# Two-layer decoder trunk on one core: the last mLSTM head takes its projection groups three to a chunk, and the mixer outputs are converted between its last chunks

## The reference, cut to what matters

```python
z = rms_norm(x, norm_g) @ w_in             # q, k, v, output gate o, gates
...
h = mlstm_chunkwise(q, k, v, li, lf)       # 4 heads, sequential over chunks
h = rms_norm(h, out_g)                     # per head
h = h * sigmoid(o)
return h @ w_out                           # the output projection
```

## Time and profile before

| | us |
|---|---|
| median of 3 runs | 2363.09 |
| lowest and highest | 2362.88 to 2363.49 |
| the profiled execution's own time | 2363.16 |
| its span | 2361.0 |

### The profile page before, as it was taken

One profiled execution on the slowest core, in us unless ns is written; L12 is line 12 of the kernel. 1 busy time (PEld: TensorE's weight loads), 2 busy tenths in 40 slices (PEclk: granted clock), 3 DMA queues, 4 the chain that ended last, 5 costly groups with the idle time before them and its releaser, 6 DMA issues.

```text
span 2361.0 us, 26713 instructions
## 1 busy us (share of the span) xinstructions
PE 2297.2 (97%) x10488; PEld 1878.4 (80%) x10488; DVE 1248.3 (53%) x1184; ACT 572.6 (24%) x854; POOL 898.7 (38%) x401
## 2 busy tenths in 40 slices
PE   6999999999999999999999999989999999999999
PEld 5777768888888888888777787778888888888887
DVE  8765684355545555555662443353645555544553
ACT  5445442211111111111333333332211111111110
POOL 2221225634344343434731322246344343443432
PEclk9999999999999999999998999999999999999999
DMA  4211103111111111111311111121111111111112
GB/s 157 61 38 35 41 19 116 45 54 45 54 44 52 45 45 53 44 54 51 116 37 57 44 61 54 36 107 46 53 45 46 52 44 53 44 53 45 46 53 81
DMA packets 36911, 131.47 MB, mean 56 GB/s; under 512 B 4568, under 2 KB 4952, under 8 KB 36832
## 3 DMA queue, kind: packets, MB, share of 16 engines
q1 hardware_dynamic: 34384, 121.72, 16.8%
q10 hardware_dynamic: 2448, 8.65, 0.9%
HBM read 117.73 MB, written 8.42 MB: 53 GB/s over the span
## 4 chain that ended last, share of the span: by engine, by line
PE 91%; DVE 4%; ACT 2%; POOL 2%; issue 1%; DMA 0%; SPq 0%; ACTq 0%; POOLq 0%; DVEq 0%
PE pj L1260 41%; PE dn L1280 17%; PE pj L324 16%; PE pj L303 6%; PE dn L1328 2%; PE dn L631 1%; PE pj L655 1%; PE pj L1328 1%; POOL ssum L389 1%; PE dn L1698 1%; PE pj L641 1%; PE dn L1726 1%; PE pj L463 1%; PE dn L1735 1%; PE dn L1729 1%
## 5 line engine op out<-in xcount | busy, mean ns | idle before, releaser
L1526 POOL TENSOR_TENSOR w_hi<-w_raw,ones 128x1024 fp32r<-128x1024 f32 x188 | 359.6, 1913 | 1421.0 <-PE pj L1260 569.5
L1528 POOL TENSOR_TENSOR w_lo<-w_raw,w_hi 128x1024 fp32r<-128x1024 f32 x188 | 474.7, 2525 | 14.8
L1369 DVE SCALAR_TENSOR_TENSOR ffn_y<-ffn_h,params,ffn_y 128x1024 f32<-128x1024 f32 x176 | 324.1, 1842 | 117.4 <-ACT ffn_y L1377 109.6
L1377 ACT ACTIVATE ffn_y<-ffn_h,params 128x1024 f32<-128x1024 f32 x88 | 109.6, 1245 | 885.5 <-DVE ffn_h L1358 885.5
L1358 DVE TENSOR_TENSOR ffn_h<-pj,rms_bc 128x1024 f32<-128x1024 f32 x88 | 107.8, 1225 | 365.1 <-PE pj L1260 351.5
L1418 DVE TENSOR_TENSOR res<-dn,res 128x1024 f32<-128x1024 f32 x144 | 176.1, 1223 | 115.4 <-PE dn L1280 115.4
L1260 PE MATMUL pj<-xa_hi,w_hi 128*128 128x512 f32 x704 | 216.9, 389 | 0.0
L1260 PE MATMUL pj<-xb_hi,w_hi 128*128 128x512 f32 x704 | 216.9, 389 | 0.0
L1260 PE MATMUL pj<-xa_lo,w_hi 128*128 128x512 f32 x704 | 216.8, 389 | 0.0
L1260 PE MATMUL pj<-xb_hi,w_lo 128*128 128x512 f32 x704 | 216.7, 389 | 0.0
L1260 PE MATMUL pj<-xa_hi,w_lo 128*128 128x512 f32 x704 | 216.7, 389 | 0.0
(11 more groups left out here) (265 smaller groups left out, 3395.0 us busy)
## 6 DMA issues: line engine op xcount, KB each, us to landing
w_raw<-weights SPq DMA_DIRECT2D x189, 512.0 KB, 3.5
x_first<-x_t SPq DMA_DIRECT2D x8, 512.0 KB, 9.6
res<-x_t SPq DMA_DIRECT2D x8, 512.0 KB, 7.4
scratch<-res ACTq DMA_DIRECT2D x8, 512.0 KB, 2.6
res<-scratch SPq DMA_DIRECT2D x8, 512.0 KB, 6.5
y_t<-res ACTq DMA_DIRECT2D x8, 512.0 KB, 2.6
q_turned<-q_raw SPq DMA_DIRECT2D x16, 128.0 KB, 2.3
k_turned<-k_raw SPq DMA_DIRECT2D x16, 128.0 KB, 2.3
```

The costliest lines, as they stand in the source:

```text
L1369: dve.scalar_tensor_tensor(y[:, :], h[:, SH - lag:SH - lag + S], f.tap(j, m, q), y[:, :], ALU.mult, ALU.add).then_inc(taps[f.l], 1)
L1377: act.activation(f.y[m][:, :], f.h[m][:, SH:SH + S], ACT.Identity, bias=f.tap(j, m, 3), scale=f.tap(j, m, 2)).then_inc(center[f.l], 1)
L1526: pool.tensor_tensor(whi[:, w, :], raw[:, r, :], ones[:, 0:1].to_broadcast([P, D]), ALU.mult).then_inc(w_high, 1)
L1528: pool.tensor_tensor(wlo[:, w, :], raw[:, r, :], whi[:, w, :].bitcast(F32), ALU.subtract).then_inc(w_ready, 1)
```

## The change

The last head takes three groups in a chunk like the other heads. Its sixteen groups then lie in the chunks 0 to 4 (three each) and 5 (one), and the chunks 6 and 7 have none. The six conversions are spread over the last three chunks: block 0 in chunk 5, blocks 1 and 2 in chunk 6, blocks 3 to 5 in chunk 7. On ACT and on DVE they stand at the end of the chunk, behind the numerator's copy and the state, and in chunk 5 also behind the sigmoid and the evacuation of `o1`. The first four groups of output 0 go to PE behind the numerators of chunk 6 (groups 0 and 1) and chunk 7 (2 and 3); `pe_out` leaves out what was given (`given`). Arithmetic and results are unchanged.

```diff
+        def pe_out_group(pe, l, X, order, d, q):
+
+            ready = (cat_hi[l], cat_lo[l], q + 1) if d == 0 else ()
+            pe_group(pe, (T_OUT0, T_OUT1)[l] + d, jobs[f"out{l}", d], X, order[q], q == 0, q == KC - 1, *ready)
+
-        def pe_out(pe, l, X, order, begun, early, before_last):
+        def pe_out(pe, l, X, order, begun, early, before_last, given=0):
...
-            for d, q in first + [(d, q) for d in range(begun) for q in range(early, KC)]:
+            for d, q in first[given:] + [(d, q) for d in range(begun) for q in range(early, KC)]:
                 if (d, q) == first[-2]:
                     before_last(pe)
-                ready = (cat_hi[l], cat_lo[l], q + 1) if d == 0 else ()
-                pe_group(pe, base + d, jobs[f"out{l}", d], X, order[q], q == 0, q == KC - 1, *ready)
+                pe_out_group(pe, l, X, order, d, q)
...
+        CAT_FROM = 5
+        CAT_AT = ((0,), (1, 2), (3, 4, 5))
+        OUT_AT = ((), (0, 1), (2, 3))
+
+        def chunk_fill(last, c):
+
+            return range(3 * c, min(3 * c + 3, 2 * KC) if last else 3 * c + 3)
...
# PE, in each chunk
-                    pe_mix1_group(pe, *side1(h, per * c))
+                    fill = chunk_fill(last, c)
+                    for G in fill[:1]:
+                        pe_mix1_group(pe, *side1(h, G))
                     if c == 0:
                         pe_ST(pe, h, c)
                     pe_num(pe, h, c)
-                    for G in range(per * c + 1, per * c + per):
+                    for G in fill[1:]:
                         pe_mix1_group(pe, *side1(h, G))
+                    if last and c >= CAT_FROM:
+                        for q in OUT_AT[c - CAT_FROM]:
+                            pe_out_group(pe, 1, XB, range(KC), 0, q)
+                            given += 1
...
# ACT, in each chunk
                     act_num(act, h, c)
-                    for G in range(per * c, per * c + per):
-                        if last and G == 15:
-
-                            act.wait_ge(tile_done, T_OUT1)
-                            for e in range(EARLY_CAT):
-                                act.wait_ge(m_cat, e + 1)
-                                act_cat(act, 1, e, XB, cat1[:, e, :])
+                    for G in chunk_fill(last, c):
                         if G in (7, 15):
                             act_sig(act, h, G // KC)
+                    if last and c >= CAT_FROM:
+                        act.wait_ge(tile_done, T_OUT1)
+                        for e in CAT_AT[c - CAT_FROM]:
+                            act.wait_ge(m_cat, e + 1)
+                            act_cat(act, 1, e, XB, cat1[:, e, :])
...
# DVE, in each chunk
-                    for G in range(per * c, per * c + per):
-                        if last and G == 15:
-                            dve.wait_ge(tile_done, T_OUT1)
-                            for e in range(EARLY_CAT):
-                                dve_cat(dve, 1, e, e, XB, cat1[:, e, :])
+                    for G in chunk_fill(last, c):
                         if G in (7, 15):
                             dve_evac1(dve, f"o{G // KC}", h)
+                    if last and c >= CAT_FROM:
+                        for e in CAT_AT[c - CAT_FROM]:
+                            dve_cat(dve, 1, e, e, XB, cat1[:, e, :])
```

More of the change, by code:

```diff
@@ L1764, in pe_layer1 @@
             pe_VT1(pe, 0, 1)
+            given = 0
             for h in range(HEADS):
                 last = h == HEADS - 1
-                per = 2 if last else 3
                 for c in range(TB):
@@ L1774, in pe_layer1 @@
                     pe_num(pe, h, c)
-                    for G in range(per * c + 1, per * c + per):
+                    for G in fill[1:]:
                         pe_mix1_group(pe, *side1(h, G))
-                for G in range(per * TB, 6 * KC if not last else 0):
+                    if last and c >= CAT_FROM:
+                        for q in OUT_AT[c - CAT_FROM]:
+                            pe_out_group(pe, 1, XB, range(KC), 0, q)
+                            given += 1
+                for G in range(3 * TB, 6 * KC if not last else 0):
                     pe_mix1_group(pe, *side1(h, G))
@@ L1786, in pe_layer1 @@
                     pe_VT1(pe, h + 1, 1)
-            pe_out(pe, 1, XB, range(KC), 2, KC - 2, lambda e: pe_HT(e, HEADS - 1))
+            pe_out(pe, 1, XB, range(KC), 2, KC - 2, lambda e: pe_HT(e, HEADS - 1), given)
             pe_ffn(pe, 1)
```

## The result

The changed kernel took 2368.24 us in the median of 20 runs (2362.06 to 2370.41), the kernel before 2363.2 us (20 runs, 2360.57 to 2363.93). The ratio is 1.0018, with a 95% interval from 1.0011 to 1.0024: slower by 0.18%. The forecast was 2367.6 us, a ratio of 1.0019. Here are the span and PE's busy time from the page of the changed kernel; its profiled execution took 2368.63 us.

The account below looks back on a forecast made before the run. PE, busy 97% of the span, was taken as the bound, losing some 5.5 us in the last head. 2363.1 us plus 4.5 (3.94 of waits at full clock, 0.6 of low clock) gave 2367.6 us, range 2363.6 to 2370.0.

Parts of the forecast that it names:

- The place and size of the waits: Last head, PE: waits of 5.13 and 1.37 us in chunk 6, 0.47 and 1.80 in chunk 7; transposes +3.94 us.
- The clock: Chunk 6's numerator after the 5.13 us wait: PE's clock falls, adding 0.6 us, within 0 to 0.95.
- A shift of 1557.77 arrives at the end whole: From the transposes of the last head's output on, both kernels run the same code, so their shift reaches the end unchanged.
- a lasting low clock: Rival: waits in chunks 6 and 7 restart the low clock, some 4.8 us in place of 0.6; 2371.8 us; 5 in 100.
- The tail: Before the transposes: the head's normalization, taking 5.55 us, stays covered by PE's output groups, by 2.1 us.
- POOL's collision: POOL's weight cut ends before conversion 0 on DVE, so it no longer stretches conversions; 1.22 us each is used.
- The 2.8 us: What POOL's weight cut cost two conversions on DVE in the kernel before; forecast as gone and priced in.
- The table load: Rival: ACT loads a table before conversion 0's copy, first wait +1.28 us; 2368.9 us; 8 in 100, including a second POOL collision.
- DVE was held up: Its rival, DVE not held up: chunk 6's scores come right behind the evacuation; transposes +0.6 us, 2363.7 us; 8 in 100.
- The stall simply goes: Rival: all conversions ready when PE asks, last head loses only two score waits; 4.1 us less, 2359.0 us; 5 in 100.

Follow-up runs that it names:

- busy_gap: Changed kernel plus five spare matmuls on PE ahead of chunk 6's numerator, in the 5.1 us gap; 2364.24 us, ratio 1.0011.
- scores_first: Changed kernel with DVE's half of conversion 0 moved behind the scores of chunk 6; 2364.94 us, ratio 1.0006.
- no_fill: Changed kernel without output groups in chunks 6 and 7, conversions left where they are; 2368.91 us, ratio 1.0025.
- gate_last: Changed kernel with evacuation and sigmoid of the last gate tile moved behind the conversions in chunk 7; 2366.78 us, ratio 1.0016.
- pool_later: Kernel before, with POOL's cut of the second output tile held back until conversion 1 is done; 2362.39 us, ratio 0.9994.
- scores_ahead: Changed kernel with gate as in gate_last, DVE's conversions all behind chunk 7's scores, output groups all behind the chunks; 2356.73 us, ratio 0.9977 to the kernel before.
- chunks_only: Changed kernel with three groups a chunk, but all six conversions in chunk 7 and all output groups behind the chunks; 2363.24 us, ratio 1.0004.

## Why the prediction was right

**The place and size of the waits.** Forecast 5.13, 1.37, 0.47 and 1.80 us at full clock. With the clock held up (busy_gap) they were 5.2 (4.46 of work and 0.78), 1.32, 0.48 and 1.76, and the stretch to the transposes 55.07 us: 3.83 more than the first profile of before, for a forecast of 3.94. That the first is DVE's queue is shown by scores_first. Against the second profile of before, 53.19, it would be 1.88: the sum stood on a profile that had caught the good case of its own stall.

**The clock.** I took 0.6 us, with 0.95 as the upper end. It was 0.95 in all four profiles of the changed kernel. This term was too small by 0.35. That it goes when the gap is filled is shown by busy_gap, in one profile.

**"A shift of 1557.77 arrives at the end whole."** Here the step failed: in all four profiles of the changed kernel the clock fell once more, 0.7 to 1.3 us after the 1.81 us wait for POOL's tile, and the end came 1.6 us later than that. In the kernel before it did so in one profile of two. That this wait brings it isn't shown: the same wait stands in all thirteen profiles, and in eight of them the clock stayed up. I had a lasting low clock as a rival, at the waits of chunks 6 and 7, and had taken the 1.81 us gap as evidence against it. In the changed kernel it didn't last there, but no_fill shows that it does when those waits have no work between them.

**The start.** The last head began 0.9 us earlier than in the profile that the sum was made on; that lies outside the change. 4.78 + 1.64 - 0.92 = 5.5 us between the two profiles, and 5.0 between the medians, for 4.5. That the sum came so near is in part luck: it left out the 1.6 us and was short by 0.35 on the clock, the early start hid 0.92 of that, and against the second profile of before the same two stretches of the changed kernel are only 2.83 and 0 us longer. What the runs bear out is the waits and their sizes, not the last half microsecond.

**The tail.** Forecast: normalization covered by 2.1 us. It took from 1553.87 to 1558.18, 4.3 us and not 5.55, since the sigmoid was no longer in it; PE came at 1561.47, so it was covered by 3.3 us.

**POOL's collision** was gone, as forecast (conversion 0 took 1.22 us), and gate_last and pool_later show it as the cause of 5.26 us for two conversions. The 2.8 us were no gain of their own: conversion 0 stood free of POOL, but behind the sigmoid.

**The rivals.** The table load didn't come. DVE was held up; made otherwise, PE's time is that of scores_first, 53.93, that is 2.7 us and not 0.6 over before: I had left out ACT's load of the exponential ahead of the numerator's copy. "The stall simply goes" is what scores_ahead reaches, by another order: I priced it at 4.1 us, and the stretch gained 3.76. The three groups a chunk by themselves (chunks_only) make the stretch 2.7 or 0.8 us longer than the two profiles of before, against 4.8 or 2.8 for the whole change, and the median shows no loss. In scores_ahead they let POOL finish its cut under bare chunks; whether it could do without them wasn't tried.

What stays open: what decides when the clock falls, and so why it came behind the 1.81 us wait in five of thirteen profiles; and where the runs of the changed kernel near 2362 us kept their clock up.

## What to carry to other kernels

Work given to a stalled engine helps only if the engines that feed it are free to release it: write out, for each in-order queue, what stands in front of the instruction that the chain waits for next, and put the short one of the chain (0.29 us of scores) ahead of the long one that has slack (1.22 us of conversion behind a sigmoid). Where a wait can't be avoided, cut it into pieces with work between them; they were worth 2 us here, by my estimate as clock and not as filled time. And cut the profiles at marks: a difference of 0.2% in the whole was blurred by 6 us of scatter ahead of the stage, while the stage of the changed kernel repeated to 0.02 us in four profiles. Take more than one profile of the kernel before as well: its stage was 51.24 us in one and 53.19 in the other, and the forecast stood on the first.

## What the runs showed of the hardware

- The clock's fall is not fixed to a gap's length: after the same 3.27 us gap it was low for 3.4 us in one execution of the kernel before, which cost next to nothing, and for 6.7 us in another, which cost 1.95; after a gap of 1.81 us it fell in five profiles of thirteen (1.6 us each).
- Matmuls whose result nobody reads (4.46 us in a gap of 5.1) held the clock at 1.00 and cost no time (busy_gap).
- An SBUF-to-SBUF subtraction of 128x1024 on DVE took 1.22 us alone and 2.91 us over POOL's weight cut, ending 1.1 us after POOL had. In pool_later POOL's two halves took 2.81 and 3.25 us under DVE's conversions, against 1.9 and 2.4. An evacuation from PSUM (1535.23, 1.22 us) over the same cut wasn't stretched. The Trainium skill (SBUF — State Buffer, section "SBUF: two separate sides") says that a GpSimd operation that reads SBUF and a DVE operation with two SBUF inputs lock a shared pair of ports against each other for a whole instruction. By it, as an estimate from the trace's durations, the conversion of gate_last would end 1.22 us after POOL's half, at 1537.97+1.22 = 1539.19; it ended at 1539.06, so the trace agrees to 0.13 us.
